# Who copies the first 128 columns of the expert activation: VectorE between two multiplies, or ScalarE

## What is computed

```python
for e in range(N_EXPERTS):
    a = jax.nn.silu(hf @ w_e_gate[e]) * (hf @ w_e_up[e])
    y = y + combine[:, e:e + 1] * (a @ w_e_down[e])
```

## Time and profile before

| | us |
|---|---|
| median of 3 runs (1366.71 to 1369.71) | 1368.7 |
| the profiled execution's own time | 1367.59 |
| its span, first to last instruction | 1365.0 |
| the expert blocks in it | about 826 to 1296 |

### The profile page before, as it was taken

How to read it: one execution, slowest core, us unless ns; L and a number is a source line. 1 busy time by engine, 2 the same in 40 slices (tenths; PEclk the granted TensorE clock), 3 DMA queues, 4 the chain that set the end, 5 groups by cost and what they waited for, 6 DMA issues and landing times.

```text
span 1365.0 us, 20069 instructions
## 1 busy us (share of the span) xinstructions
PE 1297.5 (95%) x7313; PEld 1006.2 (74%) x7314; DVE 741.6 (54%) x1025; ACT 556.0 (41%) x783; POOL 275.6 (20%) x433
## 2 busy tenths in 40 slices
PE   4999999999999989999999999999999999999994
PEld 2766678898787756656687877888888888888851
DVE  5733232334512075676777774557888141549748
ACT  0432022322212156556633252447776232447522
POOL 0132320002200066666421120000000000000053
PEclk9999999999999999999999999999999999999997
DMA  9853320102021171121432469867999261639874
GB/s 336 323 185 125 124 70 1 63 1 78 20 81 43 47 214 38 40 56 32 158 106 95 142 222 355 307 246 286 399 399 398 86 244 61 246 139 399 300 244 163
DMA packets 138920, 234.55 MB, mean 172 GB/s; under 512 B 57472, under 2 KB 59080, under 8 KB 138856
## 3 DMA queue, kind: packets, MB, share of 16 engines
q1 hardware_dynamic: 128584, 196.42, 40.5%
q0 software_dynamic: 6496, 23.60, 5.1%
q10 hardware_dynamic: 3776, 13.67, 2.5%
HBM read 197.97 MB, written 35.68 MB: 171 GB/s over the span
## 4 chain that ended last, share of the span: by engine, by line
PE 79%; POOL 7%; issue 5%; DVE 5%; DMA 2%; SPq 1%; ACT 1%; POOLq 0%; ACTq 0%; DVEq 0%
PE psum L841 73%; POOL arena L2153 5%; DMA arena<-in_w_ada_mix 2%; PE psum L1266 2%; PE psum L1068 1%; PE psum L1272 1%; DVE arena L2092 1%; DVE arena L2091 1%; PE psum L948 1%; DVE arena L2084 1%; PE psum L1162 1%; DVE arena L2083 1%; PE psum L892 1%; POOL arena L2150 0%; DMA arena<-expert_rows,smalls 0%
## 5 line engine op out<-in xcount | busy, mean ns | idle before, releaser
L841 PE MATMUL psum<-arena 128*64 128x128 f32 (+10 forms) x1540 | 169.8, 358 | 23.0 <-DMA arena<-in_w_ada_mix 14.7
L841 PE MATMUL psum<-win_high,x_low 128*128 128x512 f32 (+1 forms) x432 | 168.7, 390 | 0.0
L841 PE MATMUL psum<-win_high,x_high 128*128 128x512 f32 (+1 forms) x416 | 166.2, 400 | 0.0
L841 PE MATMUL psum<-high,h_high 128*128 128x512 f32 x416 | 162.0, 390 | 2.5 <-DVE h_low L2038 2.5
L841 PE MATMUL psum<-win_low,x_high 128*128 128x512 f32 (+1 forms) x416 | 162.4, 390 | 0.0
L841 PE MATMUL psum<-high,h_low 128*128 128x512 f32 x416 | 162.1, 390 | 0.0
L841 PEld LDWEIGHTS psum<-arena 128*64 128x64 f32 (+4 forms) x1540 | 86.0, 139 | 99.7 <-issue 71.7
L2033 DVE TENSOR_TENSOR low_odd<-raw_odd,high 128x2048 fp32r<-128x2048 f32 x48 | 107.9, 2287 | 37.5 <-ACT high L1553 37.4
L2033 DVE TENSOR_TENSOR low_even<-raw_even,high 128x2048 fp32r<-128x2048 f32 x48 | 107.8, 2286 | 37.6 <-ACT high L1553 37.2
L1873 DVE TENSOR_TENSOR_SCAN arena<-arena,psum 128x512 f32<-128x512 f32 (+3 forms) x112 | 108.2, 1003 | 19.7 <-ACT arena L1497 19.5
L2153 POOL TENSOR_TENSOR arena<-arena 128x512 f32<-128x512 f32 (+4 forms) x116 | 96.8, 835 | 9.5 <-POOL arena L2147 0.3
(11 more groups left out here) (264 smaller groups left out, 2302.4 us busy)
## 6 DMA issues: line engine op xcount, KB each, us to landing
raw_even<-in_w_e_gate SPq DMA_DIRECT2D x8, 2048.0 KB, 11.4
raw_even<-in_w_e_up SPq DMA_DIRECT2D x8, 2048.0 KB, 17.2
raw_even<-in_w_e_down SPq DMA_DIRECT2D x8, 2048.0 KB, 16.2
raw_odd<-in_w_e_gate SPq DMA_DIRECT2D x8, 2048.0 KB, 10.6
raw_odd<-in_w_e_up SPq DMA_DIRECT2D x8, 2048.0 KB, 16.8
raw_odd<-in_w_e_down SPq DMA_DIRECT2D x8, 2048.0 KB, 15.9
win<-in_w_in SPq DMA_DIRECT2D x7, 2048.0 KB, 8.1
expert_rows<-arena ACTq DMA_DIRECT2D x26, 512.0 KB, 6.2
```

The costliest lines, as they stand in the source:

```text
L841: pe_last[0] = nc.tensor.matmul(*x, **y)
```

## The change

In the experts, the copy of the first turned part (columns 0 to 127, f = 0) into `a_high` leaves ScalarE's loop. VectorE does it between its second and third multiply, after a wait for the first turn (`s_at`). It signals on a new semaphore `s_aD`, once per block; TensorE (for f = 0) and VectorE's first subtraction wait for that instead of `s_aH`. ScalarE's semaphore `s_aH` now counts two parts per block.

```diff
@@ -1276,8 +1276,10 @@
                         for f in range(FC):
                             part = [i for i, (f0, f1, _) in enumerate(act_parts) if f0 == f]
-                            if part:
-                                pe.wait_ge(s_aH, N_ACT * b + part[0] + 1)
+                            if f == 0:
+                                pe.wait_ge(s_aD, b + 1)
+                            elif part:
+                                pe.wait_ge(s_aH, (N_ACT - 1) * b + part[0])
@@ -1581,6 +1583,8 @@
                         for i, (f0, f1, at) in enumerate(act_parts):
+                            if i == 0:
+                                continue
                             act.wait_ge(s_at, N_ACT * b + i + 1)
                             A(a_high[:, f0:f1], bank(at)[:, 0:(f1 - f0) * P].rearrange(
                                 "p (f q) -> p f q", q=P), ACT.Copy).then_inc(s_aH, 1)
@@ -2053,11 +2057,17 @@
                         dve.wait_ge(s_sg, b + 1)
                         dve.wait_ge(s_gu, 2 * b + 2)
-                        for f0, f1, _ in act_parts:
+                        for i, (f0, f1, _) in enumerate(act_parts):
                             fs = slice(f0 * P, f1 * P)
                             TT(an[:, fs], sg[:, fs], bank(1)[:, fs], ALU.mult).then_inc(s_a, 1)
+                            if i == 1:
+                                dve.wait_ge(s_at, N_ACT * b + 1)
+                                V.tensor_copy(a_high[:, 0], bank(act_parts[0][2])[:, 0:P]).then_inc(s_aD, 1)
                         for i, (f0, f1, at) in enumerate(act_parts):
-                            dve.wait_ge(s_aH, N_ACT * b + i + 1)
+                            if i == 0:
+                                dve.wait_ge(s_aD, b + 1)
+                            else:
+                                dve.wait_ge(s_aH, (N_ACT - 1) * b + i)
                             TT(a_low[:, f0:f1], bank(at)[:, 0:(f1 - f0) * P].rearrange(
                                 "p (f q) -> p f q", q=P), a_high_f[:, f0:f1], ALU.subtract).then_inc(s_aL, 1)
```

More of the change, by code:

```diff
@@ L348, in stream_step @@
         s_hH, s_wH, s_wL = sem("block_h_high"), sem("weights_high"), sem("weights_low")
-        s_gu, s_sg, s_g1, s_a, s_at, s_aH, s_aL, s_yp, s_ye, s_ys = [sem(n) for n in
-            ("gate_up_ready", "gate_sig", "gate_silu", "act_ready", "act_turned", "act_high", "act_low",
+        s_gu, s_sg, s_aD, s_a, s_at, s_aH, s_aL, s_yp, s_ye, s_ys = [sem(n) for n in
+            ("gate_up_ready", "gate_silu", "act_high_by_dve", "act_ready", "act_turned", "act_high", "act_low",
              "down_ready", "y_copied", "y_stored")]
```

## The result

| | before | after |
|---|---|---|
| median, us | 1367.8 (4 runs) | 1382.59 (1378.91 to 1383.33, 4 runs) |
| profiled execution, us | 1367.59 | 1378.91 |
| its span, us | 1365.0 | 1377.1 |

The ratio is 1.0099, with a 95% interval of 1.008 to 1.0119: slower by 0.8 to 1.2% of 1368, or 11 to 16 us. The forecast was 1381.2, in a range of 1378 to 1389.

The account below looks back on a forecast made before the run. TensorE was taken to bound the expert stretch (busy 467.61 of 470 us). Delay of 0.78 less a 0.30 cushion gives 0.48 us, 26 times: 12.5 us, taking the median from 1368.7 to 1381.2, range 1378 to 1389.

Parts of the forecast that it names:

- The copy itself: Moves 26 times 0.28 us from ScalarE to VectorE; neither is in the chain, so no cost, no gain, no earlier finish.
- The third multiply 0.78 late: On VectorE, behind the copy that waits for the first turn: starts at 1073.46 instead of 1072.68, 0.20 after the copy.
- The cushion of 0.30: TensorE's idle time before a_high's load, read as waiting for ScalarE's first copy; absorbs 0.30 of 0.78, leaving 0.48 per block.
- at 1074.13: On TensorE, a_high's load follows when the last two turns' loads end, at 1074.13 instead of 1073.65: 0.48 us later.
- VectorE's slack: Low parts move 0.78 in a period growing 0.48, losing 0.30; two blocks without slack cost at most 0.6 us, none taken.
- Rival 1: The 0.30 before a_high's load is TensorE's own issue time, absorbing nothing: 26 times 0.78 is 20.3 us, so 1389.0; chance 0.09.
- Rival 2: VectorE's copy hides among the multiplies if released early enough: 2.6 us faster, 1366.1; chance 0.05 together with an unchanged 1368.7.
- Rival 3: TensorE's longer pauses in expert blocks lower its granted clock: 44 us on top of 12.5, so 1425; chance 0.03.
- The sum: Over the 26 expert blocks, 0.48 us each: 12.5 us, bringing the median from 1368.7 to 1381.2, 0.9% slower.

Follow-up runs that it names:

- the filler: Kernel before, plus one 128x128 VectorE copy from PSUM into scratch between second and third multiply, without a wait: 1368.27 us, ratio 0.9989.
- the earlier turn: First activation turn moved behind the sixth of eight row turns: ratio 0.9973 on the kernel before, 1.0047 on the changed kernel, 0.997 with VectorE copying last.
- four fillers: Kernel before, plus four 128x128 VectorE copies from PSUM into scratch between second and third multiply, without a wait: 1380.16 us, ratio 1.0084.

## Why the prediction was right, point by point

- **The copy itself costs nothing and is done no earlier.** Shown: copied by VectorE behind the third multiply, the kernel takes what it took before, and the copy starts 0.98 or 0.99 after the first multiply in either place.
- **The third multiply 0.78 late.** It was 0.79: the copy at 0.98 as forecast, the spacing behind it 0.21 where 0.20 was taken. Held to the copy's end it would have been 0.29. So the rule of the Trainium skill's "VectorE: DVE Perf Modes", section "The DRAIN you can't avoid", in its plain form doesn't hold between this copy and this multiply; the trace agrees with the exception that the page makes for an operation that isn't held.
- **The cushion of 0.30.** It was 0.34 (0.79 less 0.45). The step that was a little off is the a_high load "at 1074.13", taken as the end of the last turn's load, 0.20 after the two loads begin. It starts 0.16 after they begin. 0.48 per block was thus 0.45, inside the bounds given for it. The reading behind the cushion, that the load waits for ScalarE's copy, rested on differences of 0.04 us and less in one block; the filler and the earlier turn have shown it since.
- **VectorE's slack.** The prediction let the low parts lose 0.30 us of it, priced that at up to 0.6 us and took nothing. The price was nothing, but the step was wrong: in the one-block experts VectorE waits 0.20 to 0.37 us for TensorE ahead of the first multiply, also in the two that had no such wait. Ahead of the fourth of the five low parts behind h_low it used to wait some 0.5 us for ScalarE's high part. The delay was taken from that wait: in the block that begins at 967.16 the five run without a pause, and ahead of the two multiplies that had no wait it shrank from 0.54 to 0.20. Such a wait in the middle is slack too, and I had counted only the last one. (Ahead of one of the two, in the kernel before, ScalarE had also waited 0.53 us for weights, until 1031.95; after the change it did not.) The rows are one of before, then two of after:

```profile
1029.17 4.49 DVE L2033 TENSOR_TENSOR low_even<-raw_even,high 128x2048 fp32r<-128x2048 f32 x2 [0.54 <-ACT high L1553]
...
971.77 11.40 DVE L2037 TENSOR_TENSOR low_odd<-raw_odd,high 128x2048 fp32r<-128x2048 f32 x5
...
1034.16 4.50 DVE L2037 TENSOR_TENSOR low_even<-raw_even,high 128x2048 fp32r<-128x2048 f32 x2 [0.20 <-ACT high L1555]
```

- **Rival 1, no cushion,** fell with one filler: 0.20 of delay, no time. **Rival 2, not slower:** by the prediction it needs a copy that starts 0.48 earlier; with the earlier turn it started 0.22 earlier, the period fell by 0.23, and the change was still slower than the kernel before. **Rival 3, the clock:** 1.00 from 840 to 1280 us after the change; TensorE's pauses of 0.6 us there didn't bring it down. Of the swinging that the Trainium skill's "TensorE: Matmul & The Clock Gate", section "A second HAM failure mode: psum-queue depth-cycling", tells of, no run here shows anything in the expert stretch.
- **The sum**, 12.5 us, stands against 11.7 by the periods, 11.3 between the profiled executions and 14.8 between the medians. That the median came out within 1.4 us of the forecast (1382.59 for 1381.2) is in part luck: the blocks gave 0.8 less than the sum, the median of before was 0.9 lower than the 1368.7 that the forecast stood on, and the runs have 3.1 us that the blocks don't explain.

## What to carry to other kernels

An in-order engine that is asked to wait in the middle of a batch delays the rest of the batch, so look first at who needs what stands behind the wait: here the waiting engine held up the very operand that the engine it waited for needed next. The work moved was 0.28 us and free; its place cost 0.45 per block. Before paying for a faster copy, ask what releases it: moving the producing turn two places earlier, with the copies left alone, gained 3.7 us, which the move of the copy could not.

## What the runs showed that I had not expected

- A short copy on VectorE and one on ScalarE from PSUM to SBUF are the same to TensorE: 0.98 to 0.99 us after the first multiply the one or the other starts, and a_high's load follows 0.39 to 0.40 us after that start. I had thought that VectorE might release TensorE up to 0.06 us sooner.
- Idle time that the profile puts down to "issue" was a wait for another engine: 7.8 us of it shrank by as much as one filler delayed the turns ahead of it (from 0.30 to 0.10 a block), without moving the load. With four fillers it was gone, and only then did the load move.
